# Twelve gate chunks of a two-block transformer kernel: three products of 256 columns become one of 512 and one of 256, with the halves added on VectorE

## What is computed

```python
proj = h @ w_in                      # ... gate_logit is the last 4*1024 columns of proj
ys = _token_mixers(...)              # four branches of 256 channels each
branch = jnp.einsum('bsnc,ncd->bsnd', ys, w_branch[l])
gates = jax.nn.sigmoid(gate_logit.reshape(bsz, seq, N_BRANCH, D_MODEL))
x = x + jnp.sum(gates * branch, axis=2) @ w_out[l]
```

## Time and profile before

| | us |
|---|---|
| median of three runs | 1305.91 |
| lowest, highest | 1302.75, 1306.93 |
| the profiled execution's own time | 1305.2 |
| its span, first to last instruction | 1303.1 |

### The profile page before, as it was taken

The page is one execution under the profiler, slowest core; times in us unless marked ns, Lnnn a source line. Parts: engine busy times, 40 slices in busy tenths (PEclk is TensorE's granted clock), DMA queues, the critical chain, the costliest instruction groups (busy, mean ns, idle before and its releaser), DMA issues.

```text
span 1303.1 us, 19063 instructions
## 1 busy us (share of the span) xinstructions
PE 1225.7 (94%) x7404; PEld 1086.1 (83%) x7404; DVE 774.3 (59%) x946; ACT 598.7 (46%) x825; POOL 172.2 (13%) x175
## 2 busy tenths in 40 slices
PE   6999999998899999799998799999799987999997
PEld 6899999997788887788887688887699866888875
DVE  5744664457688544554445577763576855777642
ACT  6635654443444333354334444443476754544431
POOL 1000000013122200311010122220101101222200
PEclk9989989998899999899999899999899988999999
DMA  9343343544355555444354445554534234455530
GB/s 354 111 163 130 120 156 132 191 161 162 129 185 177 215 193 193 158 162 161 141 183 161 145 172 186 190 194 169 193 131 161 69 128 161 162 189 187 190 111 33
DMA packets 32002, 212.00 MB, mean 163 GB/s; under 512 B 4197, under 2 KB 4861, under 8 KB 7624
## 3 DMA queue, kind: packets, MB, share of 16 engines
q1 hardware_dynamic: 28936, 201.68, 43.4%
q0 software_dynamic: 2720, 9.26, 2.1%
q10 hardware_dynamic: 288, 0.23, 0.1%
HBM read 210.08 MB, written 1.07 MB: 162 GB/s over the span
## 4 chain that ended last, share of the span: by engine, by line
PE 83%; issue 6%; DVE 4%; ACT 4%; DMA 1%; POOL 1%; SPq 0%; DVEq 0%; POOLq 0%; ACTq 0%
PE acc L385 44%; PE acc L470 17%; PE acc L472 9%; PE aux L385 6%; PE acc L425 1%; PE acc L429 1%; PE acc L427 1%; DMA raw<-in_stream 1%; ACT wh L358 1%; PE aux L1993 1%; PE aux L524 1%; PE aux L2054 1%; DVE x L1464 1%; ACT ns L1025 1%; DVE wl L366 1%
## 5 line engine op out<-in xcount | busy, mean ns | idle before, releaser
L358 ACT ACTIVATE wh<-raw 128x2048 fp32r<-128x2048 f32 x190 | 364.2, 1917 | 311.3 <-PE acc L385 195.0
L366 DVE TENSOR_TENSOR wl<-raw,wh 128x2048 fp32r<-128x2048 f32 x130 | 298.0, 2294 | 288.2 <-ACT wh L358 288.0
L470 PE MATMUL acc<-hx,wh 128*128 128x512 f32 x960 | 338.3, 396 | 0.8 <-DVE hx L1375 0.8
L472 PE MATMUL acc<-hx,wl 128*128 128x256 f32 x960 | 270.4, 282 | 0.0
L385 PE MATMUL acc<-hx,wh 128*128 128x256 f32 x1280 | 240.7, 290 | 2.2 <-DVE hx L539 1.9
L470 PEld LDWEIGHTS acc<-hx,wh 128*128 128x128 f32 x960 | 181.5, 189 | 43.3 <-issue 1.9
L385 PEld LDWEIGHTS acc<-hx,wh 128*128 128x128 f32 x1280 | 206.1, 198 | 5.9 <-issue 2.9
L385 PE MATMUL acc<-hx,wl 128*128 128x256 f32 x640 | 184.4, 288 | 0.0
L472 PEld LDWEIGHTS acc<-hx,wl 128*128 128x128 f32 x960 | 183.2, 191 | 0.0
L373 DVE TENSOR_TENSOR wl<-raw,wh 128x1024 fp32r<-128x1024 f32 x120 | 154.0, 1283 | 36.2 <-ACT wh L358 36.2
L385 PEld LDWEIGHTS acc<-hx,wl 128*128 128x128 f32 x640 | 126.4, 198 | 0.0
(11 more groups left out here) (306 smaller groups left out, 1806.2 us busy)
## 6 DMA issues: line engine op xcount, KB each, us to landing
raw<-in_stream SPq DMA_DIRECT2D x190, 1024.0 KB, 4.8
bias_b<-in_bias POOLq DMA_DIRECT2D x7, 512.0 KB, 3.7
grow<-in_grows POOLq DMA_DIRECT2D x4, 512.0 KB, 4.5
nbias<-strip POOLq DMA_DIRECT2D x4, 512.0 KB, 4.3
x<-in_x SPq DMA_DIRECT2D x2, 512.0 KB, 4.1
y<-x SPq DMA_DIRECT2D x1, 1024.0 KB, 3.9
decay<-in_decay POOLq DMA_DIRECT2D x1, 512.0 KB, 3.9
growb<-in_grows POOLq DMA_DIRECT2D x1, 512.0 KB, 3.9
```

The costliest lines, as they stand in the source:

```text
L358: nc.scalar.activation(wh[:, s, :], raw[:, s, :], ACT.Copy).then_inc(hi_ready, 1)
L366: nc.vector.tensor_tensor(wl[:, s, :], raw[:, s, :], wh[:, s, :].bitcast(F32), ALU.subtract).then_inc(lo_ready, 1)
L470: nc.tensor.matmul(out[:, :], wh[:, s, cols], hx[:, k].rearrange("p a n -> p (a n)"), start=(k == 0), stop=False, skip_group_check=True)
L472: last = nc.tensor.matmul(out[:, 0:SEQ], wl[:, s, cols], hh[:, k, :], start=False, stop=(k == KT - 1), skip_group_check=True)
```

## The change

The last twelve gate chunks are computed by `product_s` in place of `product_t`. Each gives two groups instead of one, so the gates have 28 groups in place of 16. DVE's loop splits the low part in halves and after each half does a `join`, from PSUM straight into `gate`. ACT no longer reads PSUM: it waits until both joins of the chunk are done and takes the sigmoid of `gate` in place (`gate_joined`), counting on a new semaphore `gate_open`. The waits after the loop name the new groups.

```diff
-GROUP_COUNT = {"qkv": 18, "gates": 16, ...
+GROUP_COUNT = {"qkv": 18, "gates": 28, ...
-SPLIT_COUNT = {"up": 16, "ffn_in_0": 22, "ffn_in_1": 22}
+SPLIT_COUNT = {"gates": 12, "up": 16, "ffn_in_0": 22, "ffn_in_1": 22}
+        gate_open = sem("gate_open")
...
+            def gate_joined(n, g):
+
+                group_out(act, g)
+                group_out(act, g + 1)
+                pair = gate[:, bass.ds((n * 2).value, 2), :].rearrange("p k n -> p (k n)")
+                a.activation(pair, pair, ACT.Sigmoid).then_inc(gate_open, 1)
...
             with act.Fori(0, 3) as it:
                 for s in range(4):
-                    cc = At(c + 4 + s, 4, it)
-                    split_hi(act, cc + 3)
-                    gate_out(cc)
+                    split_hi(act, At(c + 7 + s, 4, it))
+                    gate_joined(At(4 + s, 4, it), At(GROUP["gates"] + 4 + 2 * s, 8, it))
...
             with dve.Fori(0, 3) as it:
                 for s in range(4):
-                    split_lo(dve, At(c + 7 + s, 4, it))
+                    cc, g = At(c + 4 + s, 4, it), At(GROUP["gates"] + 4 + 2 * s, 8, it)
+                    for sub in range(2):
+                        split_lo_half(dve, cc + 3, sub)
+                        wait(dve, mm_done if sub else sub_done, cc + 1 if sub else At(SPLIT["gates"] + s + 1, 4, it))
+                        tile = bass.ds(At(2 * (4 + s) + sub, 8, it).value, 1)
+                        join(gate[:, tile, :].rearrange("p a n -> p (a n)"), g + sub)
...
                     if n == 0:
-                        group_out(dve, GROUP["gates"] + 14)
-                        group_out(dve, GROUP["gates"] + 15)
+                        dve.wait_ge(gate_open, 12)
...
             with pe.Fori(0, 3) as it:
                 for s in range(4):
-                    product_t(pe, At(c + 4 + s, 4, it), At(g + 4 + s, 4, it), hh, hl)
+                    product_s(pe, At(c + 4 + s, 4, it), At(g + 4 + 2 * s, 8, it))
...
-                        group_out(pe, GROUP["gates"] + 15)
-                        group_out(pe, GROUP["gates"] + 14)
+                        group_out(pe, GROUP["gates"] + 27)
+                        group_out(pe, GROUP["gates"] + 26)
```

More of the change, by code:

```diff
@@ L55 @@
     N_CHUNKS += _n
-GROUP_COUNT = {"qkv": 18, "gates": 16, "branch": 0, "out": 4, "up": 32, "down": 4, "ret": 24, "ret_out": 4,
+GROUP_COUNT = {"qkv": 18, "gates": 28, "branch": 0, "out": 4, "up": 32, "down": 4, "ret": 24, "ret_out": 4,
                "ffn_in_0": 44, "ffn_out_0": 4, "nsa": 12, "nsa_out": 4,
```

## The result

The changed kernel takes 1314.45 us (median of four runs, 1312.61 to 1315.23) beside 1304.33 of the kernel before: ratio 1.0068, interval 1.0035 to 1.0102. The forecast was 1314.3 us, slower by more than 0.3%. Run again beside 11 runs of the kernel before, it gave 1.009, interval 1.0057 to 1.0123. The profiled execution took 1314.79 us, with a span of 1312.7 in place of 1303.1.

The account below looks back on a forecast made before the run. The prediction took a round of waits between ACT and DVE, 6.15 us a gate chunk, to bound the changed stage. 1305.2 + 7.7 for the stage + 1.4 for a clock dip before the branch = 1314.3 us, range 1309.0 to 1319.5.

Parts of the forecast that it names:

- The ring: In the looped gate chunks: split, half, join, half, join, sigmoid, next split on ACT and DVE close a round of 6.15 us.
- PE's price: In the gate chunks: the new form takes PE 5.55 us a chunk against 5.76, 2.5 us less for twelve.
- the 0.5 us that the prediction set beside its 2.5: Gate chunks: saving for twelve by the Trainium skill's 2.5 ns a matmul, against 2.5 us from the profile rows.
- The free round: In the gates: the case that the round does not bound the stage, 1305.3 us; same rival as Not slower, chance 0.07.
- The start: Entry to the gate loop: DVE comes at 215.81, PE waits some 1.9 us, ACT's next split is at 220.01.
- The end: After the twelfth sigmoid: ACT's copy of the attention output starts at 287.66 in place of 279.92, +7.74 us.
- The clock term: Before the branch: PE's wait of 2.2 us lowers its clock, costing 1.4 us, thought likelier than not.
- the shift stays whole: From the branch on: the old order holds and the gates' delay is kept in full, since everything downstream hangs on PE.
- The dip behind the first wait: Near 218 us: lower clock makes chunk 2 up to 1.7 us longer, nearly hidden, taken as nothing.
- Not slower: Rival in the gates: engines overlap more than start distances say, so the round is not the bound; 1305.3 us, chance 0.07.
- An oscillating clock: Rival in the gates: PE's 0.6 us idle per chunk makes its clock swing; about 1339 us, chance 0.05.
- The longer ring: Rival in the gates: register addresses before the joins make the round 6.35 us; 1316.6 us, chance 0.10.

Follow-up runs that it names:

- e1_lag: Changed kernel with ACT taking each chunk's sigmoid one pass later, behind the split of the chunk four ahead; 1306.28 us, ratio 1.002.
- e3_ring_plus: Changed kernel with one more DVE reduction into scratch (0.60 us) before each second join; 1321.02 us in a single run.
- e5_lag_plus: e1_lag with the added DVE reduction of e3_ring_plus; 1307.47 us in a single run.
- e2_join_first: Changed kernel with each DVE join placed before its half of the low split instead of behind it; 1306.35 us, ratio 1.0005.
- e7_early_dve: Changed kernel with the last part of the attention output on DVE moved behind the first looped chunk's two joins; 1308.97 us in a single run.
- e4_static: Changed kernel with ACT's loop written out, so that its addresses and wait counts are constants; 1311.36 us in a single run.
- e8_lag_again: The same kernel as e1_lag, executed once more; 1307.78 us.

## Why the prediction was right

**The ring** was the step that carried it, and it held: forecast 6.15 us, measured 6.22. By parts, from the round shown: split to half 1.94 (forecast 1.95), half to join 1.14, join to half 0.60, half to join 1.13 (1.14), join to sigmoid 0.88 (0.82), sigmoid to split 0.53 (0.50). The 0.07 lie around the sigmoid in place: it begins 0.06 later, and the split behind it 0.03 later, than the nearest rows had it. e1_lag and e3_ring_plus show the cause from both sides, e5_lag_plus that it is the order and not the load.

**PE's price** of the new form, 5.55 us against 5.76, is one of two: it was read in `ffn_in_0`, and the `up` stage of the same trace has 5.65. So the gain of the wider matmuls is 1.3 or 2.5 us for twelve chunks, and the 0.5 us that the prediction set beside its 2.5 is below both. The ring hid the difference. The free round, which was the rival's case, was well priced: the rival put it at 1305.3 us, and e1_lag and e2_join_first measured 1306.28 and 1306.35.

**The start**: DVE's first half to ACT's second split, forecast 4.20, measured 221.33 - 217.04 = 4.29. PE's wait was put at 1.9 us and was 3.0: PE's first looped chunk, without a dip in this execution, ended at 215.9 (forecast 215.8), but DVE came to its loop 1.2 us later than before. The ring starts from DVE, so the length of PE's wait changed nothing. e7_early_dve prices the late start at 2.8 us.

**The end**: from DVE's first looped half to the ysh copy, forecast 71.85 (287.66 - 215.81), measured 289.85 - 217.04 = 72.81; before 64.11. That makes + 8.7 us for the stage, where the sum had + 7.7: eleven rounds of 0.07 or 0.08 and 0.1 at the start.

**The clock term failed.** The sum put 1.4 us on a dip before the branch. In neither profile of the changed kernel was there one, after waits of 2.30 us; nor in e7_early_dve after 2.20; e4_static had one after 2.00 and e3_ring_plus after 3.39. The price was 1.5 us in e4_static, near the 1.4, but about 2.6 in e3_ring_plus, where the clock was 0.50 from 296 to 302 us (first 24 matmuls 5.46, next 24 3.08, against 3.11 and 2.88). The dip had been thought likelier than not, and the length of the wait does not settle whether it comes: PE waits 2.02 us for `ysl` in the second block in both kernels, and before the clock fell, while the changed kernel has it at 1.00 from 1079.45 to 1082.95 us.

**What made up for it.** In the sum the place of the dip was taken by the 1.0 of ring and start, and in the profiled pair by 1.2 us that came before the loop: DVE reached it at 217.04 instead of 215.81, in code that the change does not touch. Behind the branch the forecast's "the shift stays whole" did not hold either: the shift is 7.35 us at one place and 9.59 at another, and the slower pace of `ffn_in_0` and of `ffn_in_1` put in 2.2 us each in the changed kernel's profile. What the change does is shown by the stage, 8.7 us longer; that the total came within 0.2 us of the forecast is luck.

The dip behind the first wait came as written and cost 0.06 us in one profile (226.20 - 225.01 = 1.19 from half to second join, not 1.13), 0.37 in the other.

**The rivals.** Not slower: the five distances of starts left no overlap. An oscillating clock: PE stops for its bank in most chunks, and yet the granted clock is full over the whole stretch (changed kernel, columns as above):

```profile
226.00:288.00 62.00, 59.14 (x332) 1.00 0.48 169
```

The Trainium skill (TensorE: Matmul & The Clock Gate, section "A second HAM failure mode: psum-queue depth-cycling") tells of another kernel, in bf16, in which short idles between groups make the clock swing. This trace does not agree: at about half a microsecond in 6.2 (two matmul pairs 0.92 us apart instead of 0.35) it shows none of it. So the rival fell, but one argument against it was wrong. Not all dips of the trace before follow waits of 2 us or more; the one in the first looped gate chunk has none above 0.94 us close ahead of it (timeline; stretch as above):

```profile
205.71 3.36 PE L385 MATMUL aux<-v_b,pt_b 128*128 128x64 f32 x24 [0.94 <-ACT pt_b L811]
```

```profile
208.00:210.00 2.00, 2.00 (x11) 0.50 0.11 33
```

The longer ring, 6.35: the joins' register addresses cost nothing: from half to join it is 1.14 us, as in the rows, and 1.13 to 1.15 in e7_early_dve, where the first joins have constant addresses.

## What to carry to other kernels

Before giving an engine's product more readers, write down each engine's order within one pass and look for a round: a wait on one engine, behind work that waits for what is queued behind that wait. Its length is the sum of start distances and does not depend on how idle the engines look (here 3.78 and 2.66 us of idle in 6.22). Take the reading that closes the round one pass late, or put it first. Here that took the loss away (1.002 and 1.0005) but left no gain. The gain of the wider matmuls, 0.1 or 0.2 us of 5.76 a chunk, showed in the time only when the late start and the tail were gone too (0.9977). And don't read a price of 0.1 us from one stage of one trace: look whether another stage gives the same.

## What the runs showed of the hardware that was not expected

The same matmul pairs (512 and 256 columns) run at one of two paces at full granted clock: 5.55 us for 32 matmuls or 5.65. The same program had 5.65 in one execution and 5.55 in the next (e1_lag, e8_lag_again), and within one execution the pace changes between stages, but in none of these profiles inside one. What decides it was not found. Over the 22 chunks of such a stage it is worth 2.2 us, more than the whole gain of the wider matmuls at the slower pace.

A sigmoid of 128x512 in place in SBUF takes 0.63 us, from PSUM 0.60. With its address and wait counts as constants ACT started the sigmoid 0.10 us sooner after the join (e4_static).

The start of the looped chunks lay between 206.9 and 211.8 us in the eleven profiles, with the same code in front. Differences of 3 us between single executions of this program are not the edit's; a stretch inside one trace separates them.
